# One-core diffusion step with 32 experts: the last expert pair's rows spread over the tokens by a one-hot matmul, the other rows read back during that pair

## The chip, the cores and the metric

The kernel runs on one core of one Trainium2 chip. The metric is device time in microseconds (us), the median of several runs. The core's engines are named as in the profile: PE (TensorE matmul), PEld (its weight loads), DVE (VectorE), ACT (ScalarE), POOL (GpSimd) and SP (SyncE, which here only issues DMAs). Everything is fp32. One fp32 matmul stands in the trace as two MATMUL records, a transpose as one.

## The reference, cut to what matters

384 tokens (128 context, 256 latent) of width 1024 pass two layers. Layer 0 mixes tokens by attention, layer 1 by a Hyena long convolution whose filters are computed from small weights. Each layer ends with a mixture of 32 experts, of which every token uses two. What the change touches is the sum over experts and what follows it:

```
combine = jnp.sum(jax.nn.one_hot(expert_id, N_EXPERTS) * e_w[..., None], axis=1)
a = jnp.einsum('nd,edh->neh', t, w_gate)
b = jnp.einsum('nd,edh->neh', t, w_up)
act = jax.nn.silu(a) * b * combine[:, :, None]
out = jnp.einsum('neh,ehd->nd', act, w_down)
...
x = x + g2 * hierarchical_moe(h, ...)        # then the next layer's RMSNorm, or the final one
```

## The kernel before, in words

**Tokens and experts.** The residual `xT` lies transposed, 8 chunks of 128 features by 384 tokens. The experts are worked in 16 pairs, `q` = 0 to 15; a pair has 128 slots, 64 for each expert, and a slot holds one token of that expert. A table `tab` in SBUF gives each slot its token, its weight and its row of the buffer `yD` in HBM ("expert_rows", 768 rows of 1024: two for each token). A slot with no token has a number out of range. A pair with more than 64 tokens for an expert gets extra windows, run by `extra(q)` under a branch.

**One pair** (`moe` of each engine). PE runs `gate_up` (L849, 16 matmuls of 512 columns), ACT the Silu (L1230), DVE the product `A` (L1655), PE transposes it (L855), DVE copies it (`AT`, L1658), PE runs `down` (L863, 8 matmuls), and ACT and DVE copy the halves of the result to `Y` (L1238, L1667). POOL scatters `Y` to its rows of `yD` by an indirect DMA (`scatter`, L1811) and gathers tokens for later pairs (L1806, L1839). Meanwhile PE turns the next pair's gathered tokens.

**The end of a layer's experts.** After the last pair's scatter SP reads all of `yD` back in eight DMAs of 384 KB (`load_rows`, L429) into `y2`, two rows for each token. Per chunk of features, DVE adds the two rows (L1682, counted by `ysum`), PE transposes the sum (three transposes, L941), DVE adds it, gated, to `xT` (`add_mix`, L1421), ACT squares the new chunk (L1125), and PE adds the square to the norm's sum by a matmul with ones (`norm_sum`, L628). Then ACT takes the root (L1127), DVE the reciprocal (L1389 after layer 0, L1404 at the end of the kernel) and the normalised chunks (L1391, L1406).

**Filters beside the experts, layer 0 only.** The Hyena filters are made in 8 pieces, `f` = 0 to 7, one in every two pairs. SP loads a piece's weights and decays (`load_filter`, L391 to L394); ACT makes the decays (`decay`, L1087, L1094) in even pairs; in odd pairs PE makes the taps in three parts (`taps`, L582), DVE multiplies them by the decay (`tap_decay`, L1357) and forms sums and differences (`tap_sums`, L1363, L1365), ACT takes absolute values (L1100) and POOL adds them (`size_sums`, L1872, L1874); in the next even pair PE makes the spectra in three parts (`spectra`, L599 to L604) and the sizes (`sizes`, L613), and ACT and DVE copy the spectra out. Piece 7 has no next pair: its spectra and sizes stand between the last pair and the residual. The sums and differences lie in `hT`, which the next norm overwrites.

**After layer 0** the Hyena input projection follows: 24 steps of 8 matmuls of 384 columns (L997). Its weights come in six chunks of 2 MB (`load_win`, L434) into the ring where the expert weights were; step `n` uses chunk `n // 4`, and a semaphore stands for one or two chunks (`WIN_GROUP`).

**What sets the order.** Every engine runs its own list in program order, and semaphores join the lists. On SP the end of layer 0 is:

```
sp.wait_ge(sem("gu_mm"), PAIRS - 1)
for n in (0, 1):
    load_win(sp, n)
sp.wait_ge(sem("dn_mm"), 2 * (PAIRS - 1))
load_win(sp, 2)
load_rows(sp, 0)
```

A wait on one list holds all that stands behind it there.

## Time and profile before

| | us |
|---|---|
| three runs, median (lowest to highest) | 1273.88 (1272.04 to 1278.01) |
| the profiled execution, own time | 1280.37 |
| its span, first to last instruction | 1278.5 |
| PE busy in it | 1089.1 (85%) |
| DVE, ACT, POOL busy | 476.8, 257.0, 185.4 |

The profiled execution took 6.5 us longer than the median run, and 1.9 us of it lie around the span. Busy shares average over stages with different limits, so the stages are read one by one: the chain of waits says what ended last in each, the timeline what else ran, and the tables by stage how fast PE's clock and the DMAs were. Times within the trace count from the start of the span.

### The profile page before, as it was taken

Reading aid. Unit: us, or ns where it says so; the run is one execution under the profiler, and the core shown is the slowest. Engines: PE = TensorE matmul, PEld = TensorE weight load, DVE = VectorE, ACT = ScalarE, POOL = GpSimd, SP = SyncE. Lnnn points to the kernel's source line nnn. Section 1 sums busy time; section 2 is a strip of 40 time slices with the busy share of each in tenths; the row PEclk is TensorE's granted clock in tenths of the full one; section 3 lists DMA queues with packets and bytes.
Section 4 is the critical chain, followed back from the end, with each engine's and each line's share of the span. In section 5 each row is a group of like instructions: output and inputs, shape, how many; then the busy total and the mean of one; then the engine's idle time right before and its main releaser. Section 6 shows DMA issues by size and latency. Waiting matters only on the chain.

```text
span 1278.5 us, 14637 instructions
## 1 busy us (share of the span) xinstructions
PE 1089.1 (85%) x5429; PEld 574.4 (45%) x5429; DVE 476.8 (37%) x1014; ACT 257.0 (20%) x498; POOL 185.4 (15%) x209
## 2 busy tenths in 40 slices
PE   5799888987999789999879999989765988878864
PEld 3344555555444234443345565658662422222223
DVE  3355556234233113332263336784540111111116
ACT  2211334022333123223231110000221000000001
POOL 1020000002322023221100002130011222222100
PEclk8899989986999899999889999999967989889997
DMA  9996985532899569999870200505320899999943
GB/s 351 404 322 264 251 294 225 227 132 70 313 395 401 228 238 356 398 406 410 305 286 1 99 1 0 230 1 198 154 94 20 325 413 413 413 412 407 407 161 129
DMA packets 94241, 324.54 MB, mean 254 GB/s; under 512 B 17647, under 2 KB 33423, under 8 KB 77380
## 3 DMA queue, kind: packets, MB, share of 16 engines
q1 hardware_dynamic: 71936, 303.49, 61.3%
q0 software_dynamic: 15504, 13.37, 3.4%
q10 hardware_dynamic: 6708, 6.45, 1.4%
q8 instruction: 58, 0.95, 0.3%
q14 instruction: 35, 0.29, 0.1%
HBM read 333.22 MB, written 30.11 MB: 284 GB/s over the span
## 4 chain that ended last, share of the span: by engine, by line
PE 63%; DMA 19%; DVE 7%; issue 4%; ACT 3%; SPq 3%; POOL 0%; ACTq 0%; another core or an unknown queue 0%; POOLq 0%; DVEq 0%
PE bank L849 15%; DMA ring<-in_moe_w_up 10%; PE bank L997 10%; PE bank L863 6%; PE bank L668 3%; PE bank L1036 3%; PE bank L784 3%; DMA ring<-in_w_ada 3%; DMA hT<-in_hy_log_decay 3%; PE bank L564 3%; PE bank L599 2%; PE bank L1025 2%; PE bank L983 2%; DMA ring<-in_moe_w_down 2%; PE bank L796 2%
## 5 line engine op out<-in xcount | busy, mean ns | idle before, releaser
L849 PE MATMUL bank<-ring,work 128*64 128x512 f32 x1120 | 267.5, 633 | 44.3 <-issue 38.2
L849 PEld LDWEIGHTS bank<-ring,work 128*64 128x64 f32 x1120 | 82.5, 145 | 220.6 <-issue 216.4
L863 PE MATMUL bank<-ring,work 128*64 128x512 f32 x560 | 129.4, 604 | 4.3 <-DVE work L1643 1.5
L997 PE MATMUL bank<-hT,ring 128*128 128x384 f32 x384 | 128.0, 494 | 5.3 <-ACT hT L1134 5.3
L1655 DVE SCALAR_TENSOR_TENSOR work<-bank,work 128x256 f32<-128x256 f32 x32 | 15.5, 484 | 261.3 <-ACT work L1230 248.6
L997 PEld LDWEIGHTS bank<-hT,ring 128*128 128x128 f32 x384 | 74.0, 194 | 58.0 <-issue 9.7
L863 PEld LDWEIGHTS bank<-ring,work 128*64 128x64 f32 x560 | 37.5, 138 | 74.1 <-issue 63.4
L1230 ACT ACTIVATE work<-bank 128x256 f32<-128x256 f32 x32 | 12.3, 383 | 249.8 <-PE bank L849 249.8
L1667 DVE COPY work<-bank 128x512 f32<-128x512 f32 x32 | 22.1, 692 | 106.8 <-PE bank L863 106.8
L1806 POOL DMA_INDIRECT work<-token_vectors,work x28 | 28.7, 1026 | 199.6 <-PE bank L832 185.7
L564 PE MATMUL bank<-ring,condS 128*32 128x256 f32 x768 | 48.6, 408 | 10.0 <-DVE ada L1334 5.5
L1811 POOL DMA_INDIRECT expert_rows<-work x32 | 32.0, 1000 | 114.9 <-DVE work L1667 113.0
L599 PE MATMUL bank<-hT,const 128*128 128x256 f32 x160 | 43.8, 409 | 4.6 <-DVE hT L1365 4.6
L1036 PE MATMUL bank<-work,ring 128*128 128x128 f32 (+1 forms) x256 | 42.2, 327 | 1.7 <-DVE work L1757 1.7
L668 PE MATMUL bank<-hT,ring 128*64 128x384 f32 x256 | 43.0, 489 | 0.0
L784 PE MATMUL bank<-work,ring 128*128 128x384 f32 x128 | 41.5, 487 | 0.7 <-DVE work L1499 0.7
L1270 ACT ACTIVATE work<-bank,pc 128x128 f32<-128x128 f32 (+1 forms) x48 | 17.6, 418 | 119.8 <-PE bank L997 119.8
L1238 ACT ACTIVATE work<-bank 128x512 f32<-128x512 f32 x32 | 19.1, 598 | 111.5 <-PE bank L863 111.5
L1036 PEld LDWEIGHTS bank<-work,ring 128*128 128x128 f32 x256 | 38.4, 190 | 5.5 <-issue 2.1
L1729 DVE TENSOR_SCALAR work<-work,pc 128x385 f32<-128x385 f32 x24 | 11.5, 480 | 76.6 <-ACT work L1270 76.6
L1125 ACT ACTIVATE sq<-xT 128x384 f32<-128x384 f32 x38 | 19.7, 522 | 100.9 <-DVE xT L1421 59.2
L564 PEld LDWEIGHTS bank<-ring,condS 128*32 128x32 f32 x768 | 24.8, 116 | 33.4 <-DVE ada L1334 9.0
(269 smaller groups left out, 1481.5 us busy)
## 6 DMA issues: line engine op xcount, KB each, us to landing
ring<-in_moe_w_gate SPq DMA_DIRECT2D x32, 2048.0 KB
ring<-in_moe_w_up SPq DMA_DIRECT2D x32, 2048.0 KB
ring<-in_moe_w_down SPq DMA_DIRECT2D x32, 2048.0 KB
ring<-in_w_ada SPq DMA_DIRECT2D x24, 2048.0 KB, 12.5
ring<-in_hy_w_in SPq DMA_DIRECT2D x6, 2048.0 KB, 20.4
filter_spectra<-work ACTq DMA_DIRECT2D x8, 768.0 KB
work<-expert_rows SPq DMA_DIRECT2D x16, 384.0 KB, 6.7
ring<-filter_spectra SPq DMA_DIRECT2D x2, 3072.0 KB, 12.1
```

Source lines behind the costliest of these rows:

```text
L564: last = mm(ada_bank(t)[32 * j:32 * j + 32, 0:256], condS[:, 4 * hk + k, :], w[:, k, 256 * j:256 * j + 256], start=(hk == 0 and k == 0), s ...
L599: last = mm(dst, m[:, off:off + P], smdf[:, part if part < 2 else r, c, :], start=(j == 0), stop=(j == len(ops) - 1))
L668: last = mm(bank[m % 2][b * HD:(b + 1) * HD, 0:T], wq[:, k, h * HD:(h + 1) * HD], hT[:, k, :], start=(k == 0), stop=(k == KD - 1))
L784: last = mm(bank[m % 2][:, 0:T], wo[:, k, m * P:(m + 1) * P], oT[:, k, :], start=(k == 0), stop=(k == KD - 1))
L796: last = mm(bank[c][:, 0:NG + NE], hT[:, k, c * P:(c + 1) * P], rout[:, l, k, :], start=(k == 0), stop=(k == KD - 1))
L849: last = mm(bank[2][WIN * j:WIN * (j + 1), :], gt[:, k, WIN * j:WIN * (j + 1)], gu[:, :, j, k, :], start=(k == 0), stop=(k == KD - 1))
L863: last = mm(bank[b + hf][WIN * j:WIN * (j + 1), :], AT[:, k, WIN * j:WIN * (j + 1)], dn[:, j, k, hf * HALF:(hf + 1) * HALF], start=(k == 0 ...
L983: last = mm(b[:, :], m[:, off:off + P], ztok[o][:, c, hf * HALF:(hf + 1) * HALF], start=(j == 0), stop=(j == len(ops) - 1))
L997: last = mm(bank[n % 2][:, 0:T], w[:, k, (n % 4) * P:(n % 4 + 1) * P], hT[:, k, :], start=(k == 0), stop=(k == KD - 1))
L1036: last = mm(bank[4 + m % 2][:, lo:hi], wout[:, k, m * P:(m + 1) * P], st[:, 2, k, a0:a1], start=(k == 0), stop=(k == KD - 1))
L1806: ind(out=G[:, q % 2, :], out_offset=None, in_=hD, in_offset=at_rows(tab[:, 4 * q + 1:4 * q + 2]), bounds_check=T - 1, oob_is_err=False).t ...
L1811: ind(out=yD, out_offset=at_rows(tab[:, 4 * q:4 * q + 1]), in_=Y[:, q % 2, :], in_offset=None, bounds_check=2 * T - 1, oob_is_err=False).t ...
```

## The change

**Rows.** Only 15 pairs scatter. Pair 15's result stays in SBUF, in `Y[:, 1]`. DVE makes a one-hot matrix of 128 slots by 384 tokens from the slots' token numbers (`spread_last`, during pair 13, into `rstd`), and PE spreads the pair's rows over the tokens by one matmul of 384 columns for each chunk of features (`last_rows`). Into the same PSUM bank it adds the other rows by three matmuls with the identity (`other_rows`) in place of three transposes. The chunks take seven banks instead of two. The buffers are moved so that `y2` does not lie over `Y[:, 1]` and `GT`; SP reads the rows back as soon as pair 14's scatter has landed and pair 15's extra windows are done (`rows_done`), and DVE adds the first four chunks of rows before it copies pair 15's result. As pair 15's rows of `yD` are no longer written, POOL first writes zeros over all of it, three DMAs of 1 MB at the start of each layer's experts.

**Filters.** Piece 7's last tap part comes before pair 15's `down`; its sums go to the ring where pair 14's down weights were; `tap_sums` comes after the residual on DVE; spectra parts 0 and 1 after the residual on PE; part 2 and the sizes after step 1 of the input projection. The copies and the store follow in the projection.

**Loads.** SP issues chunk 0, the row read, chunks 1 and 3, waits for the last spectra and sizes, then chunks 2, 4 and 5.

**Root table.** `squares` begins with a Sqrt of one column, which loads ACT's table for it. Some semaphores are merged (`wo_in` and `wout_in` into `proj_in`, `kv_out` into `y_out`).

```
@@ layout
-        Y = ws(5120, 2 * D).rearrange("p (b d) -> p b d", b=2)
-        GT = ws(7168, D).rearrange("p (k s) -> p k s", k=KD)
-        Gx = ws(8192, D)
...
+        Gx = ws(5120, D)
+        GTx = ws(6144, D).rearrange("p (k s) -> p k s", k=KD)
+        Yx = ws(7168, D)
+        Y = ws(8192, 2 * D).rearrange("p (b d) -> p b d", b=2)
+        GT = ws(10240, D).rearrange("p (k s) -> p k s", k=KD)
...
+        smdf_last = ring[:, 8192:9728].rearrange("p (d t c) -> p d t c", d=2, t=3)
+        RES_BANK = [0, 1, 2, 4, 5, 6, 7]
-        WIN_GROUP = [0, 0, 1, 2, 2, 3]
+        WIN_GROUP = [0, 0, 1, 1, 2, 2]
@@ SP
-            for s in range(2):
-                sp.wait_ge(S_(f"scat{s}_"), B_(f"scat{s}_") + 16 * (PAIRS // 2))
+            sp.wait_ge(S_("scat0_"), B_("scat0_") + 16 * (PAIRS // 2))
+            sp.wait_ge(S_("scat1_"), B_("scat1_") + 16 * (PAIRS // 2 - 1))
+            sp.wait_ge(S_("rows_done"), B_("rows_done") + 1)
...
+            load_win(sp, 0)
+            load_rows(sp, 0)
+            load_win(sp, 1)
+            sp.wait_ge(sem("gu_mm"), PAIRS)
+            load_win(sp, 3)
+            sp.wait_ge(sem("cf_mm"), 3 * NF)
+            sp.wait_ge(sem("size_mm"), NF)
             load_win(sp, 2)
+            load_win(sp, 4)
             sp.wait_ge(sem("dn_mm"), 2 * PAIRS)
             load_win(sp, 5)
@@ PE
+                    if l == 0 and q == PAIRS - 1:
+                        taps(q // 2, 2)
...
+                def last_rows(k):
+                    mm(bank[RES_BANK[k % 7]][:, 0:T], Y[:, 1, k * P:(k + 1) * P], rstd[:, :], start=True, stop=True)
+
+                def other_rows(k):
+                    pe.wait_ge(S_("ysum"), B_("ysum") + k + 1)
+                    for c in range(TC):
+                        last = mm(bank[RES_BANK[k % 7]][:, c * P:(c + 1) * P], y2[:, 0, c, k * P:(k + 1) * P], ident,
+                                  start=False, stop=True, skip_group_check=True)
+                    last.then_inc(S_("res_mm"), 1)
+
+                pe.wait_ge(S_("spread"), B_("spread") + 1)
+                pe.wait_ge(S_("y_set"), B_("y_set") + 2 * PAIRS)
...
+                for k in range(KD - 1):
+                    last_rows(k)
                 for k in range(KD):
+                    if k == 3:
+                        pe.wait_ge(S_("moe_add"), B_("moe_add") + 2)
+                        last_rows(KD - 1)
+                    other_rows(k)
                     if k >= 2:
                         norm_sum(n_norm + 1, k - 2)
                 for k in (KD - 2, KD - 1):
                     norm_sum(n_norm + 1, k)
+                if l == 0:
+                    pe.wait_ge(S_("moe_add"), B_("moe_add") + 2 * KD)
+                    for part in range(2):
+                        spectra(NF - 1, part)
...
+                if n == 1:
+                    spectra(NF - 1, 2)
+                    sizes(NF - 1)
@@ ACT
+                fn(idle[:, :], eps_col[:, :], ACT.Sqrt)
                 for k in range(KD):
                     act.wait_ge(sem(x_set), base + step * (k + 1))
@@ DVE
+                def spread_last():
+                    at = 4 * (PAIRS - 1) + 1
+                    link(v.tensor_copy(mx[:, 0, 0:1], tab[:, at:at + 1]))
+                    for c in range(TC):
+                        link(v.tensor_scalar(mx[:, 1, c:c + 1], mx[:, 0, 0:1], float(PAIRS), float(-c * P * PAIRS), ALU.mult, ALU.add))
+                    for c in range(TC):
+                        last = v.tensor_scalar(rstd[:, c * P:(c + 1) * P], C["slotrow"], mx[:, 1, c:c + 1], None, ALU.is_equal)
+                    last.then_inc(S_("spread"), 1)
...
+                    if l == 0 and q == PAIRS - 1:
+                        tap_decay(q // 2, 2)
+                    if q == PAIRS - 1:
+                        for k in range(KD // 2):
+                            row_sum(k)
                     dve.wait_ge(S_("dn_mm"), B_("dn_mm") + 2 * q + 2)
...
+                for k in range(KD):
+                    add_mix(k, bank[RES_BANK[k % 7]], S_("moe_add"), ada[:, l, 5], S_("res_mm"), B_("res_mm"))
+                    if k < KD // 2:
+                        row_sum(KD // 2 + k)
                 if l == 0:
+                    tap_sums(NF - 1)
@@ POOL
+                pool.wait_ge(S_("g_clear"), B_("g_clear") + 2)
+                for i in range(TC):
+                    pool.dma_start(yD.rearrange("(c p) d -> p c d", p=P)[:, 2 * i:2 * i + 2, :], G).then_inc(S_("zero_in"), 16)
...
-                pool.wait_ge(S_("g_clear"), B_("g_clear") + 2)
+                pool.wait_ge(S_("zero_in"), B_("zero_in") + 48)
...
+                    if q == PAIRS - 1:
+                        nc.gpsimd.nop().then_inc(S_("rows_done"), 1)
...
-                scatter(PAIRS - 1)
```

**How it moves instructions.** A row is a line of the kernel, its operation, output, inputs, output shape and count. On PE, pair 15 of layer 0 and what follows it was, before (gate-up L849, taps L582, spectra L599 to L604, sizes L613, row transposes L941, norm sum L628):

```order
L849 MATMUL bank<-ring,work 64x512 x16
L582 MATMUL bank<-sq,hd 128x512 x2
L855 MATMUL bank<-const,work 128x128 x2
L863 MATMUL bank<-ring,work 64x512 x8
L582 MATMUL bank<-sq,hd 128x512
L599 MATMUL bank<-hT,const 128x256 x6
L602 MATMUL bank<-hT,const 1x256
L599 MATMUL bank<-hT,const 128x256 x4
L604 MATMUL bank<-work,const 1x256
L613 MATMUL bank<-const,hT 128x1 x4
L941 MATMUL bank<-const,work 128x128 x9
L628 MATMUL bank<-sq,const 128x384
```

The same place now (taps L595, down L876, `last_rows` L946, `other_rows` L951, norm sum L641):

```order
L862 MATMUL bank<-ring,work 64x512 x16
L595 MATMUL bank<-sq,hd 128x512 x2
L868 MATMUL bank<-const,work 128x128 x2
L595 MATMUL bank<-sq,hd 128x512
L876 MATMUL bank<-ring,work 64x512 x8
L946 MATMUL bank<-rstd,work 128x384 x7
L951 MATMUL bank<-const,work 128x128 x9
L641 MATMUL bank<-sq,const 128x384
L946 MATMUL bank<-rstd,work 128x384
L951 MATMUL bank<-const,work 128x128 x3
```

The third tap part stands before the down product, the spectra and sizes are gone from here, and seven spread products stand between the down product and the first rows. The spectra (L612, L615, L617) and sizes (L626) stand now, on PE, around the first two steps of the input projection (L1025):

```order
L641 MATMUL bank<-sq,const 128x384 x3
L612 MATMUL bank<-ring,const 128x256 x6
L615 MATMUL bank<-ring,const 1x256
L612 MATMUL bank<-ring,const 128x256 x2
L1025 MATMUL bank<-hT,ring 128x384 x16
L612 MATMUL bank<-ring,const 128x256 x2
L617 MATMUL bank<-work,const 1x256
L626 MATMUL bank<-const,ring 128x1 x4
```

Two parts come before step 0 and the third, with the sizes, after step 1. On SP the end of layer 0 was, before (filter loads L391 to L394, projection weights L434, row read L429):

```order
L391 DMA hT<-in_hy_log_decay 128x256
L393 DMA sq<-in_hy_filt_w 64x256
L394 DMA sq<-in_hy_filt_b 1x256
L434 DMA ring<-in_hy_w_in 128x8x512 x3
L429 DMA work<-expert_rows 128x3x256 x8
L434 DMA ring<-in_hy_w_in 128x8x512 x3
L506 DMA ring<-filter_spectra 128x6144
```

And it is now:

```order
L403 DMA hT<-in_hy_log_decay 128x256
L405 DMA sq<-in_hy_filt_w 64x256
L406 DMA sq<-in_hy_filt_b 1x256
L447 DMA ring<-in_hy_w_in 128x8x512
L442 DMA work<-expert_rows 128x3x256 x8
L447 DMA ring<-in_hy_w_in 128x8x512 x5
L520 DMA ring<-filter_spectra 128x6144
```

One weight chunk stands before the row read instead of three, and five behind it.

## Rows read from the trace of the kernel before

**Rows 1.** Chain of waits, end of layer 0: start us, us, engine and line.
```profile
621.34 5.15 PE bank L863 x16
626.48 1.07 PE bank L582 x2
...
628.30 1.83 DVE hT L1363 x2
...
652.96 0.52 ACT sq L1125
...
655.48 2.56 DVE rstd L1389
```

**Rows 2.** Chain of waits, whole run, input projection.
```profile
659.79 90.71 PE bank L997 x272
751.37 5.16 PE bank L997 x16
```

**Rows 3.** Chain of waits, end of layer 1 and of the kernel.
```profile
1239.22 0.70 DVE work L1667
...
1240.69 2.63 DMA expert_rows<-work
...
1244.85 6.64 DMA work<-expert_rows
...
1260.76 1.28 ACT L1127
...
1262.73 2.56 DVE rstd L1404
```

**Rows 4.** Chain of waits: 12 identity-sized fp32 matmuls; gated add of one chunk.
```profile
998.17 2.68 PE bank L825 x24
...
1256.47 0.74 DVE xT L1421 x2
```

**Rows 5.** Timeline, pairs 14 and 15 of layer 0: start us, us, engine, line, form.
```profile
599.17 1.89 PE L599 MATMUL bank<-hT,const 128*128 128x256 f32 x8
...
607.68 1.13 PE L599 MATMUL bank<-hT,const 128*128 128x256 f32 x4
...
609.30 0.99 POOL L1811 DMA_INDIRECT expert_rows<-work  x1 [14.57 <-DVE work L1667]
...
610.25 7.09 PE L849 MATMUL bank<-ring,work 128*64 128x512 f32 x32
```

**Rows 6.** Timeline, norms: one norm sum; one sum of rows on DVE.
```profile
1258.22 0.81 PE L628 MATMUL bank<-sq,const 128*128 128x384 f32 x2
1258.25 0.55 DVE L1682 TENSOR_TENSOR work<-work 128x384 f32<-128x384 f32 x1
```

**Rows 7.** Busy time by stage: window, us, PE, PEld, DVE, ACT, POOL, clock, DMA, GB/s.
```profile
620.00:624.00 4.00, 3.10 (x10) 1.02 (x12) 1.94 (x4) 0.00 (x0) 0.00 (x0) 0.62 1.06 401
...
632.00:636.00 4.00, 3.88 (x9) 3.16 (x10) 0.07 (x1) 0.06 (x1) 0.65 (x1) 0.50 0.24 66
```

**Rows 8.** The instructions of line L1365: durations ns min/median/max.
```profile
L1365 DVE TENSOR_TENSOR hT<-work x8: 418/2035/2043, 351.3 to 630.0; 128x256 f32<-128x256 f32 x8
```

**Rows 9.** Instructions on expert_rows: landing of its scatters and reads.
```profile
DMA to landing us min/median/max: 2.6/6.3/7.9
```

**Rows 10.** Page, DMA issues: projection weights, KB each, median us to landing.
```profile
ring<-in_hy_w_in SPq DMA_DIRECT2D x6, 2048.0 KB, 20.4
```

**Rows 11.** Timeline of POOL, start of the experts, layers 0 and 1.
```profile
272.82 0.95 POOL L1791 MEMSET work<- 128x1024 f32 x1
...
319.56 1.07 POOL L1845 DMA_INDIRECT work<-token_vectors,work  x1 [3.51 <-DMA work<-slot_table]
...
916.90 0.95 POOL L1791 MEMSET work<- 128x1024 f32 x1
...
962.97 1.07 POOL L1806 DMA_INDIRECT work<-token_vectors,work  x1 [3.23 <-DMA work<-slot_table]
```

**Rows 12.** Timeline, first layer's start: PE's wait for adaLN weights.
```profile
60.30 2.83 PE L564 MATMUL bank<-ring,condS 128*32 128x256 f32 x32 [2.06 <-DMA ring<-in_w_ada]
```

More of the change, by code:

```diff
@@ L346, in build, with smd_of, hsum_of, sabs_of @@
         XT_BANK = [0, 1, 2, 6]
+        RES_BANK = [0, 1, 2, 4, 5, 6, 7]
+        def smd_of(f):
+            return smdf_last if f == NF - 1 else smdf
+        def hsum_of(f):
+            return hsum_last if f == NF - 1 else hsum
+        def sabs_of(f):
+            return sabs_last if f == NF - 1 else sabs
         def chunk_dst(m, lo, hi):
@@ L612, in sizes @@
                         col = 480 + 16 * o + 4 * n + 2 * j + L
-                        last = mm(bank[3][:, col:col + 1], sabs[:, L, j * P:(j + 1) * P], ones[:, 0:1], start=True, stop=True)
+                        last = mm(bank[3][:, col:col + 1], sabs_of(f)[:, L, j * P:(j + 1) * P], ones[:, 0:1], start=True, stop=True)
                 last.then_inc(sem("size_mm"), 1)
@@ L923, in moe @@
                     down(s, 4, S_("dn_mm"))
-                    if l == 0 and q % 2 == 1:
+                    if l == 0 and q % 2 == 1 and q < PAIRS - 1:
                         taps(q // 2, 2)
@@ L1242, in moe @@
                             store_spectra(q // 2 - 1)
-                    if l == 0 and q % 2 == 1:
+                    if l == 0 and q % 2 == 1 and q < PAIRS - 1:
                         sizes(q // 2)
-                if l == 0:
-                    spectra(NF - 1)
-                    store_spectra(NF - 1)
             moe(0, 1)
@@ L1252, in _ @@
             modulate(2, 1, 0)
+            spectra(NF - 1)
             def z_copy(o, g):
@@ L1732, in _ @@
                     .then_inc(sem("conv_done"), 1)
+                if n == 1:
+                    spectra(NF - 1)
+                if n == 3:
+                    filter_sizes()
                 for g in Z_TURNS_AFTER.get(n, ()):
```

84 lines of the change are left out of this document (34 added, 50 removed).

## Prediction

> **What bounds the kernel now.** I read the chain of waits first, because the change works at two ends that only the chain shows: the end of layer 0's experts and the end of the kernel. The timeline and the table by stage come second, to see what runs beside the chain there and at which clock.
>
> At the end of the kernel the chain is a plain relay [rows 3]: DVE's copy of the last pair starts at 1239.22, its rows are scattered to HBM (2.63 us), all rows are read back (6.64 us), and only then come the sums. The reciprocal of the last norm starts at 1262.73, so 23.5 us after the copy. PE does no products for the experts in that time.
>
> At the end of layer 0 the chain goes another way [rows 1]. The same scatter and read run, but the chain runs over the filters' last piece: the third tap part (626.48), sums on DVE (1.83 us for two, at 628.30), spectra and sizes on PE, and then the residual, whose last add ends at 652.96. The reciprocal starts at 655.48 and the input projection at 659.79 [rows 2]. From the start of the last down product (621.34) to the projection that is 38.5 us. Part of it is slow clock: in the 4 us from 632 PE has 0.50 of its clock, which is 1.2 GHz of 2.4, after it stood still [rows 7]. The projection starts slow too: its first 17 groups take 90.71 us, where a group at full clock takes 5.16 us, so 87.7 for 17 [rows 2]. 3.0 us are lost there.
>
> **The change part by part.**
>
> *New end of the experts, both layers.* The pieces on PE, at full clock:
> - A 384-column product takes 5.16 / 8 = 0.645 us [rows 2]. Seven come before the first rows: 4.5 us; the eighth 0.65.
> - The other rows of a chunk are three 128-column fp32 products. Twelve such take 2.68 us [rows 4], so 0.67 for a chunk and 5.4 for eight. Three transposes were cheaper, a record each instead of two.
> - Five norm sums stand before the last chunk's rows: 5 x 0.645 = 3.2 us.
>
> That makes 13.75 us on PE. Before it stands the copy (0.70 [rows 3], with a hand-over 0.74), behind it the last gated add (0.74 [rows 4]), its square (0.52 [rows 1]), its norm sum (0.81 [rows 6]) and the root. The root's table load is gone from here: after the load ended at 1260.76 + 1.28 = 1262.04 the root and hand-over took 0.69 to the reciprocal [rows 3]. The sum is 0.74 + 13.75 + 0.74 + 0.52 + 0.81 + 0.69 = 17.25 us from the start of the copy to the reciprocal. DVE's list would take 8 x 0.74 + 4 x 0.55 = 8.1 us [rows 4, 6] against PE's 9.25 after the first seven products, so PE paces it; if the two overlapped better than I lay them out, DVE's pace would give back 1.1 us in each layer.
>
> *Layer 1 alone:* 23.5 - 17.25 = **6.3 us less**. The sums of the first four chunks must not hold the copy: on DVE they stand ahead of it. Pair 14's scatter is issued about when pair 15's gate-up begins (609.30 and 610.25 in layer 0 [rows 5]); that gate-up of 7.09 us, the steps to the down product and that product lie between. Landing of scatters and reads has a median of 6.3 us and a maximum of 7.9 [rows 9], so a scatter and the read of the first columns take some 12 us and end about when the down product does. I put nothing for it.
>
> *Layer 0.* Four terms.
> 1. The third tap part now stands before the down product, and waits for the first tap multiply: about 0.7 on DVE (the size of the copy in [rows 3]) and 1.07 on PE [rows 1], 1.8 us. In return the down product begins later on a clock that is rising (0.62 in the 4 us from 620 [rows 7]), and it took 5.15 us at that clock. I take 1.3, between 0.7 and 1.8. The copy, which follows the down product's end at 626.49, starts at 627.8.
> 2. POOL's adds of absolute values now fall on the row sums that stand before the copy. One DVE sum of 256 columns took 418 ns once and 2035 ns in the median, when POOL's adds ran [rows 8]; so 0 to 1.6 us, and I take 0.8: copy at 628.6. By the Trainium skill, SBUF — State Buffer, section "Practical consequences" of its port rules, a VectorE instruction with two SBUF inputs blocks against a GpSimd one that reads SBUF, and one with a single SBUF input does not; by that the copy from PSUM itself is not held, and the sum stays; without it the copy could be held as well, which would add up to 1.6 us to the sum.
> 3. The residual's last add then ends at 628.6 + 0.74 + 13.75 + 0.74 = 643.8, against 652.96. DVE's sums for the last spectra follow: 1.83 [rows 1] + 0.42 (uncontended, [rows 8]) = 2.25 us. The root is ready after 0.52 + 0.81 + 0.69 = 2.0, so the sums cost the reciprocal 0.25: it starts at 646.1. From reciprocal to projection it is 659.79 - 655.48 = 4.3 us, so 650.4. Beside it PE runs spectra parts 0 and 1: 1.89 for the first [rows 5], as much for the second and 0.6 for its extra product, 4.4 us from 646.1, so 650.5. Both end together; the projection starts at 650.5, **9.3 us** earlier.
> 4. PE has then been busy up to the start, so I expect the full clock and the 3.0 us back. Part 2 and the sizes go into the projection, which PE bounds: 610.25 - 607.68 = 2.6 us [rows 5].
>
> Layer 0: 9.3 + 3.0 - 2.6 = **9.7 us less**.
>
> *Loads.* The row read of layer 0 starts after pair 14's scatter, issued at 609.30 [rows 5]: landed by 612 to 617, the first halves of the read by 615 to 625 [rows 9], while DVE needs them from 624 to 627. I put nothing, with the upper bound in the rivals. Behind it come projection chunks 1 and 3; two chunks at the 401 GB/s of [rows 7] take 10.5 us, well before 650. Chunks 2, 4 and 5 are issued at about 663 and step 8 needs chunk 2 at 650.5 + 2.6 + 8 x 5.16 = 694; landing took 20.4 us [rows 10], so about 10 us are spare.
>
> *Zeros.* POOL's first gather waits for 3 MB of zeros. Between the end of the memsets and that gather lie 45.8 us in layer 0 and 45.1 in layer 1 [rows 11]; 3.1 MB at some 400 GB/s are 8 us, twice that beside weight loads. What is queued behind on POOL, the slot table's scatter and read, needs the router's result, which DVE makes meanwhile. Nothing.
>
> *Root table at the first norm.* There the load (1.28 us, with its one-column Sqrt about 1.4) stands before the squares, so PE's first products start 1.4 later. But PE then waits 2.06 us for adaLN weights at 60.30 [rows 12], which covers PE's own delay. Nothing, and 1.4 at worst, if those weights are late by as much. The Trainium skill, ScalarE: Activation LUTs, "What ACT_TABLE_LOAD costs", gives 2.66 us for a switch, load and drain, which would make that bound 2.8; the trace shows 1.28 and the next instruction 0.7 later, so I keep 1.4. In the other norms the load lies under waits.
>
> Pair 13's one-hot (seven small DVE instructions) lies under the next gate-up of 7.09 us [rows 5].
>
> **The sum.** 6.3 + 9.7 = 16.0 us. The profiled execution's own 1280.37 us would be 1264.4; on the median of the runs shown, 6.5 us lower, it is 1273.88 - 16.0 = **1258 us**.
>
> **The rivals.**
> - *The first norm pays.* The request for the next adaLN weights waits for PE's first products, and if it comes 1.4 us late, so may those weights. Against it speak the 2.06 us only if PE's part alone is late. It gives 1259.4. By the skill's price it would be 1260.7.
> - *The read holds DVE in layer 0.* The row sums stand ahead of the copy on DVE, and everything hangs on the copy. The DMAs are full there (401 GB/s), and a projection chunk takes 20.4 us to land. Were the read as slow, from 617 to 637 or 638, the copy would start some 9 us late: 1267. For it: that load; against: 7.9 us was the longest of its own kind.
> - *The clock stays low.* If PE's waits in the new end are long enough for the clock to fall, the 3.0 us stay lost and the spread takes longer: 1261 to 1264.
> - *Slower: the zeros hold POOL.* A wait of the gathers takes the place of the wait removed. The slowest landing on that buffer, 7.9 us for 0.5 MB [rows 9], is 66 GB/s; at that rate 3.1 MB take 48 us and end 2 or 3 us after the gathers want to start, in each layer. The change turns to a loss where they take over 53 us (8 us late, twice). At 50 GB/s it is 63 us, 17 late in each layer: 1258 + 35 = 1293. Against it: those landings are of single scatters, whose fixed part counts in full, and the zeros go in order.
>
> That the change would not do what it says I can exclude for the order: the one-hot, the read and the spectra stand where the diff puts them.
>
> **How the numbers follow.** Forecast 0.60; first norm 0.14; read holds DVE 0.14 (about half of it less than 0.5% below the time before); clock 0.07; zeros 0.05. A measurement of this kernel can tell about 0.5%, 6.4 us, from no change. Faster by more: 0.60 + 0.14 + 0.07 + 0.07 = 0.88; the same: the other 0.07; slower: 0.05. The low end: the lowest run shown is 1.8 under the median, DVE's pace gives 2.2, the POOL collision 0.8 and the tap part 0.6: 1252. The high end takes in the first two rivals: 1267.
>
> **What would show it.** Right: no scatter and no read between the last copy and the last norm; seven products of 384 columns right after the copy, at full clock; reciprocal 17 us after the copy in layer 1 and the projection about 29 us after the start of pair 15's transposed product in layer 0; no table load there. Wrong: a DVE wait for the row read ahead of the last copy; a POOL wait for the zeros ahead of the first gather; a longer wait at the projection's steps 8 or 16.

## The result, and the profile after

The change makes the kernel faster, by less than forecast: 1264.93 us (median of 13 runs) against 1273.88 for the kernel before (13 runs beside them). The ratio is 0.9924, 95% interval 0.9906 to 0.9942, which is 9.7 us (7.4 to 12.0) where 16 were forecast; the two medians alone differ by 9.0. A second set of timings gave 0.9942 (0.9920 to 0.9963), 7.4 us. One later run of the kernel before took 1783.98 us at a granted clock of 0.59 and enters no comparison. The profiled execution took 1264.05 us, span 1262.2. It lies near its median, while the one of the kernel before lay 6.5 us over its own; so the difference of the two spans, 16.3 us, is not the gain.

**End of layer 0.** The chain of waits of the changed kernel (start us, us, engine and line), to set beside [rows 1, 2]:

```profile
616.87 2.08 PE bank L595 x2
618.94 5.92 PE bank L876 x16
624.86 0.84 issue
625.70 4.75 PE bank L946 x14
...
640.10 0.74 DVE xT L1455 x2
640.84 1.73 DVE ring L1397 x2
...
647.47 11.35 PE bank L1025 x32
...
661.19 77.51 PE bank L1025 x240
```

The scatter, the read, the last tap sums and the first spectra are gone from between the down product and the adds. The seven one-hot products (L946, two records each) follow the copy, the last add ends at 640.84, and the projection starts at 647.47, 28.5 us after the start of the down product (38.5 before; the forecast was about 29). The clock is full there, as the table by stage shows (window, us, PE, PEld, DVE, ACT, POOL, clock, DMA share, GB/s), where [rows 7] had 0.50:

```profile
632.00:636.00 4.00, 3.86 (x24) 2.90 (x23) 3.76 (x10) 1.89 (x4) 0.00 (x0) 1.00 0.92 336
```

**End of layer 1.** The same view, to set beside [rows 3]:

```profile
1215.04 3.63 DMA expert_rows<-work
...
1220.15 6.29 DMA work<-expert_rows
...
1226.94 0.55 DVE work L1697
1227.49 0.67 DVE work L1723
...
1228.29 4.75 PE bank L946 x14
1233.04 0.68 PE bank L951 x6
...
1235.19 0.88 PE bank L641 x2
...
1245.67 2.56 DVE rstd L1438
```

The chain still runs through a scatter and a read, but they are pair 14's, and they lie beside pair 15. The last sum ahead of the copy (L1697) ends 0.05 to 0.1 us after the down product does. So the copy was held by almost nothing here, though the view names the read; in the second profile of the changed kernel it starts 0.3 us after the down product's end, held by the read (run 7 has the other profiles). From the copy (1227.45) to the reciprocal (1245.67) it is 18.2 us, against 23.5 before and 17.25 forecast.

**The front.** The chain of the first norm:

```profile
18.05 0.10 ACT condS L1107
...
18.17 1.28 ACT L1147
...
29.67 1.91 PE bank L577 x32
...
31.59 0.37 SPq L394
...
46.50 16.62 DMA ring<-in_w_ada
...
63.16 3.05 PE bank L577 x32
```

The root's table load stands on the chain, as the first rival had it: behind it come the squares, PE's first adaLN products, SP's requests that wait for those, and the weights, which PE gets at 63.16 instead of 60.30 [rows 12].

**The zeros.** POOL's timeline (start us, us, engine, line, form, idle time before and its releaser) in layer 0:

```profile
274.95 2.16 POOL L1851 DMA_DIRECT2D expert_rows<-work  x3 [0.30 <-POOL work L1848]
305.05 1.06 POOL L1855 DMA_INDIRECT slot_table<-pay,idx  x1 [27.94 <-DVE pay L1625]
...
319.96 1.08 POOL L1905 DMA_INDIRECT work<-token_vectors,work  x1 [3.24 <-DMA work<-slot_table]
```

The page's DMA issues give the zeros 15.8 us to land:

```profile
expert_rows<-work POOLq DMA_DIRECT2D x6, 1024.0 KB, 15.8
```

In layer 0 the last of them lands at 293.1, 11.9 us before the first request for the slot table; in layer 1 it is 8.5 us before. The first gather waits for the slot table, and starts 0.4 us later than in [rows 11].

### The profile page after: what moved, and what is told of

Same layout as the page of the kernel before. It is cut to its first block, busy times and chain, and to the rows that moved or that the text cites. A ratio compares the mean times of both kernels' runs of the same rounds, so it can differ in the third digit from the quotient of the medians.

```text
span 1262.2 us, 14809 instructions
## 1 busy us (share of the span) xinstructions
PE 1096.0 (87%) x5509; PEld 580.6 (46%) x5509; DVE 478.0 (38%) x1028; ACT 257.5 (20%) x503; POOL 187.4 (15%) x213
## 4 chain that ended last, share of the span: by engine, by line
PE 67%; DMA 19%; DVE 5%; issue 4%; ACT 3%; SPq 2%; POOL 0%; ACTq 0%; POOLq 0%; DVEq 0%
PE bank L862 15%; DMA ring<-in_moe_w_up 12%; PE bank L1025 10%; PE bank L876 6%; PE bank L681 3%; PE bank L1067 3%; PE bank L797 3%; DMA ring<-in_w_ada 3%; PE bank L577 3%; PE bank L612 2%; PE bank L1056 2%; PE bank L1011 2%; DMA ring<-in_moe_w_down 2%; PE bank L809 2%; PE bank L838 2%
## 5 line engine op out<-in xcount | busy, mean ns | idle before, releaser
L862 PE MATMUL bank<-ring,work 128*64 128x512 f32 x1120 | 268.1, 634 | 42.2 <-issue 36.1
L876 PE MATMUL bank<-ring,work 128*64 128x512 f32 x560 | 130.2, 608 | 3.7 <-DVE work L1677 1.5
L1025 PE MATMUL bank<-hT,ring 128*128 128x384 f32 x384 | 126.3, 488 | 0.0
L1025 PEld LDWEIGHTS bank<-hT,ring 128*128 128x128 f32 x384 | 72.2, 190 | 51.9 <-ACT hT L1166 2.3
L876 PEld LDWEIGHTS bank<-ring,work 128*64 128x64 f32 x560 | 37.7, 139 | 75.5 <-issue 65.6
L1067 PE MATMUL bank<-work,ring 128*128 128x128 f32 (+1 forms) x256 | 42.2, 327 | 1.7 <-DVE work L1814 1.7
L1847 POOL MEMSET work<- 128x2048 f32 x2 | 3.6, 1806 | 240.2 <-DVE xT L1455 183.8
## 6 DMA issues: line engine op xcount, KB each, us to landing
expert_rows<-work POOLq DMA_DIRECT2D x6, 1024.0 KB, 15.8
```

What stands on the lines that cost most here:

```text
L862: last = mm(bank[2][WIN * j:WIN * (j + 1), :], gt[:, k, WIN * j:WIN * (j + 1)], gu[:, :, j, k, :], start=(k == 0), stop=(k == KD - 1))
L876: last = mm(bank[b + hf][WIN * j:WIN * (j + 1), :], AT[:, k, WIN * j:WIN * (j + 1)], dn[:, j, k, hf * HALF:(hf + 1) * HALF], start=(k == 0 ...
L1025: last = mm(bank[n % 2][:, 0:T], w[:, k, (n % 4) * P:(n % 4 + 1) * P], hT[:, k, :], start=(k == 0), stop=(k == KD - 1))
L1067: last = mm(bank[4 + m % 2][:, lo:hi], wout[:, k, m * P:(m + 1) * P], st[:, 2, k, a0:a1], start=(k == 0), stop=(k == KD - 1))
```

## The experiments

For all runs I compare stretches of the program, since two profiles of the kernel before alone differ by 7.4 us in their spans. Each number is the difference of two start times in the trace of that run, or runs from the start or to the end of its span.

| stretch, us | before | before again | changed | changed again | turned, added |
|---|---|---|---|---|---|
| second Silu to first square | 0.10 | 0.10 | 1.62 | 1.62 | 0.10 |
| start to attention's out-projection | 228.72 | 224.83 | 229.60 | 228.83 | 228.37 |
| attention's out-projection to pair 15's gate-up, layer 0 | 381.53 | 378.43 | 376.93 | 379.49 | 378.44 |
| pair 15's gate-up to projection | 49.54 | 48.97 | 40.86 | 40.92 | 35.94 |
| of it, copy to reciprocal | 28.95 | 29.11 | 18.17 | 18.18 | 14.00 |
| projection to hyena's out-projection | 211.44 | 211.46 | 212.02 | 212.05 | 212.05 |
| pair 15's gate-up to the end, layer 1 | 52.02 | 52.28 | 47.49 | 47.06 | 42.96 |
| of it, copy to reciprocal | 23.51 | 23.74 | 18.22 | 18.21 | 14.07 |

**1. The kernel before, profiled again.** No edit.

> The kernel before, profiled a second time, unchanged. My theory: its first profiled execution (1280.37 us, 6.5 over the median of its timed runs) was slow by chance in stretches that the change doesn't touch, above all the start of layer 0's experts (3.7 us, with a 1.9 us wait of DVE at 311.94 that PE's end doesn't explain). Then a second profile lies within 2 us of 1273.9, the time from the start of the out-projection of attention to the first gate-up of layer 0 is 3 to 4 us shorter (82.5 instead of 86.2), and the two tails that the change touches stay as they were: from pair 15's gate-up to the projection 49.5 us in layer 0, from pair 15's gate-up to the end 52.0 us in layer 1, both within 1 us. Rival: the stretches outside the tails are the same in every execution of the kernel before (within 0.5 us), the change itself shortens them, and 16 us was the right size for this execution: then the second profile shows 86 us again there.

The median is 1271.2 us, the profiled execution took 1272.97, span 1271.1. With no change made, the stretch from attention's out-projection to pair 15 is 3.1 us shorter and the front ahead of it 3.9 us, while both tails agree within 0.6 us with the first profile. From the out-projection to the first gate-up it is 84.2 us, 2.0 less than in the first profile, where I expected 3 to 4. One wait shows where 1.9 us of the 3.1 lay. This is DVE's copy for the first pair, in the timeline of the first profile of the kernel before:

```profile
311.94 0.69 DVE L1627 COPY work<-bank 128x512 f32<-128x512 f32 x1 [3.42 <-remote]
```

and in its second profile:

```profile
306.13 0.69 DVE L1627 COPY work<-bank 128x512 f32<-128x512 f32 x1 [1.49 <-PE bank L825]
```

The theory holds in kind: the surplus of the first profile was chance, and lies outside the tails. More than half of the 7.4 us lies in the front, where the change adds the table load, so gains and costs there can't be read from one profile of each kernel.

**2. The changed kernel again.** No edit.

> The changed kernel once more, unchanged, with a second profile. My theory, from the segments of the eight profiles so far: against the kernel before, from pair 15's gate-up to the projection 8 to 10 us less in layer 0 (39.4 to 41.0 us against 49.0 to 49.5), from pair 15's gate-up to the end 3.4 to 5.3 us less in layer 1 (47.0 to 49.1 against 52.0 to 52.3), 0.55 us more in the projection, up to 2 us more at the front; 10 to 12 us in all, ratio 0.990 to 0.9925. Rival, the sum of the prediction: 16 us, ratio 0.9875.

1265.07 us, ratio 0.9942 (0.9920 to 0.9963). The stretches come out as expected: 8.0 to 8.7 us less in layer 0, 0.6 more in the projection, 4.5 to 5.2 less in layer 1. The timed gain, 7.4 us (4.7 to 10.2), is under the 10 to 12 expected. The sum of 16 us lies outside both intervals.

**3. No early table load at the first norm.**

```
+                if n > 0:
-                fn(idle[:, :], eps_col[:, :], ACT.Sqrt)
+                    fn(idle[:, :], eps_col[:, :], ACT.Sqrt)
```

> The changed kernel, with the root's table loaded ahead at the four later norms only. My theory: at the first norm the load is 1.28 us on the chain, because ACT goes from the second Silu straight to the first square; without it the first square follows the second Silu within 0.1 us, and the root's load (1.28 us) begins at the last square's end and stands out behind PE's last product by 0.3 to 0.4 us, as in the kernel before. The first product of the ada weights then starts 0.9 us nearer to the first Silu, and so do the arrival of the last w_ada transfer that is asked for in the first 35 us (63.1 in the changed kernel) and the first q/k projection: 0.9 us less in all, ratio to the kernel before 0.9917 against the 0.9924 of the changed one. Rival, that of the prediction: PE's idle time of 2.06 us ahead of the ada products hides the load, and all of the 2.9 us shift at the front was chance: then the arrival of w_ada does not move against the first Silu, and the time is that of the changed kernel.

1260.54 us, ratio 0.9905 (0.9879 to 0.9930). The first square follows the Silu at once, and the load stands between last square and root (timeline of ACT):

```profile
16.93 0.20 ACT L1107 ACTIVATE condS<-pc 128x8 f32<-128x8 f32 x1
17.03 0.92 ACT L1158 ACTIVATE sq<-xT 128x384 f32<-128x384 f32 x2
...
24.33 1.28 ACT L1160 ACT_TABLE_LOAD   x1
```

The weights arrive at 59.1 instead of 63.2, and against the second Silu 42.2 us after it instead of 45.2. The direction is the theory's; the size, 3 us, is more than the 0.9 expected, and the clock has a share in it (the squares' products took 7.7 us here and 8.8 in the changed kernel, where PE had stood idle for 3.72 us ahead of them instead of 2.44, and the granted clock was 0.50 from 20 to 26 us; here it was back at 1.00 from 21). Run 5 bears on the rest. The two intervals of the ratio overlap; the trace decides here, not the time.

**4. No early load at all.**

```
-                fn(idle[:, :], eps_col[:, :], ACT.Sqrt)
```

> The changed kernel without any of the five early loads of the root's table. My theory: the load comes back between last square and root at the two layer ends and at the end of the kernel; there the last square and PE's last product end about 0.8 to 1.0 us apart (1243.98 and 1244.9 in the changed kernel), so that 0.3 to 0.5 us of the 1.28 stands out at each of the norms 2 and 4, and up to 0.5 at the norms 1 and 3, against 0.9 us gained at the first norm: between -0.9 and +0.9 us against the changed kernel, +0.1 as one number; copy of pair 15 to reciprocal in layer 1: 18.6 instead of 18.2. Rival: the whole load of 1.28 us stands out at each layer end, as the prediction's sum had it in its steps: 19.5 there, and +1.6 to +4 us in all.

1260.62 us, ratio 0.9913 (0.9886 to 0.9939). Copy to reciprocal is 18.5 us in both layers instead of 18.2, so an early load at a layer's end is worth 0.3 us and not 1.28 (18.6 were expected). The timeline of the end shows why:

```profile
1237.47 2.46 PE L641 MATMUL bank<-sq,const 128*128 128x384 f32 x6
...
1238.45 0.52 ACT L1156 ACTIVATE sq<-xT 128x384 f32<-128x384 f32 x1 [0.79 <-DVE xT L1454]
1238.99 1.28 ACT L1158 ACT_TABLE_LOAD   x1
1240.29 0.58 ACT L1158 ACTIVATE rstd<-bank,eps_col 128x384 f32<-128x384 f32 x1
```

The load starts as soon as the last square is done, beside the product that the root waits for. It sticks out by 0.3 us.

**5. The Silu table loaded ahead instead.** As run 3, and:

```
             act.wait_ge(sem("preset"), 3)
+            fn(idle[:, :], eps_col[:, :], ACT.Silu)
             act.wait_ge(sem("pc_done"), 1)
```

> The changed kernel without the root's early load at the first norm, and with one Silu on a spare element before ACT waits for the parameters, so that the table that it needs is loaded while ACT is idle. My theory: the first Silu then starts with DVE's copy of the parameters instead of 1.28 us behind it, and the first square 0.3 us behind that copy instead of 1.5 (0.1 and 1.28 in the kernel before, 1.6 and 1.28 in the changed one); the first ada products come 1.3 us earlier against that copy than in the run without the first early load, and 2.2 us earlier than in the changed kernel. In all 1.3 us less than without the first early load, 2 to 3 us less than the changed kernel: ratio to the kernel before about 0.990 (0.9865 to 0.992). Rival: the last w_ada transfer is bound by the queue of loads and not by the products that free its place; then its arrival does not move and the gain ends in TensorE's idle time ahead of it: 0 us.

1262.98 us, ratio 0.9902 (0.9879 to 0.9925), against 0.9905 in run 3: no gain over it. The ratio lies in the range that the theory gave, but no timing here can tell 1.3 us; by the trace the theory falls and its rival holds. The chain of waits:

```profile
25.11 0.37 SPq L394
...
26.07 7.95 SPq L469
...
44.63 15.17 DMA ring<-in_w_ada
...
59.84 1.93 PE bank L577 x32
```

PE's first products are over at 25.1 instead of 28.0 (run 3), but one of SP's requests (L469) takes 7.95 us to issue instead of 4.41, and the request for the adaLN weights that PE waits for next goes out at 44.15 instead of 43.48. In all twelve profiles it goes out between 43.5 and 44.2 where the first products end before 29.3, eight times; and 14.4 to 15.3 us after them where they end at 30.6 to 31.6, four times (45.5 to 46.1). Those four all have the early load. So the front has a floor that the queue sets, the kernel before stood on it, and the early load lifts it off in four of six runs: 1.3 us in the mean (45.1 for the six profiles with the load, 43.8 for the six without). Attention's out-projection starts 1.4 us later in the mean of the same six (227.6 against 226.2), but each six spread over 3 to 5 us there.

**6. The zeros written twice.** A second pass behind the first:

```
+                pool.wait_ge(S_("zero_in"), l * 96 + 48)
+                for i in range(TC):
+                    pool.dma_start(yD.rearrange("(c p) d -> p c d", p=P)[:, 2 * i:2 * i + 2, :], G).then_inc(S_("zero_in"), 16)
...
-                pool.wait_ge(S_("zero_in"), B_("zero_in") + 48)
+                pool.wait_ge(S_("zero_in"), B_("zero_in") + 96)
```

> The changed kernel, with the row buffer zeroed twice in each layer, one pass after the other (3.1 MB more for each layer, and POOL waits for the first pass before it issues the second). My theory: zeros cost nothing: POOL issues them at 274.95 and has no other work until 305.05, one pass lands in 15.8 us, and so two are over by about 307; the weights of the first pairs are asked for early enough. Expected: 0 to +1.5 us against the changed kernel (part of it POOL's wait at 305), and the first gate-up of layer 0 unmoved within 0.5 us. Rival: they share the transfer rate of about 415 GB/s with the weights that the first pairs wait for, and 3.1 MB at that rate are 7.6 us: then each layer's first gate-up comes up to 7 us later and the kernel takes up to 15 us more, and the one pass in the changed kernel would have eaten as much of its gain.

1262.80 us, ratio 0.9927 (0.9902 to 0.9953), the same as the changed kernel. POOL's timeline, layer 0:

```profile
271.87 2.16 POOL L1851 DMA_DIRECT2D expert_rows<-work  x3 [0.30 <-POOL work L1848]
290.10 2.10 POOL L1854 DMA_DIRECT2D expert_rows<-work  x3 [16.08 <-DMA expert_rows<-work]
301.97 1.07 POOL L1858 DMA_INDIRECT slot_table<-pay,idx  x1 [9.77 <-DVE pay L1625]
```

POOL waits for the first pass and is still 9.8 us early. From the out-projections to the first gate-up it is 82.1 and 100.1 us (82.5 and 100.0 in the changed kernel). The zeros cost nothing, and the rival that had them hold POOL is out.

**7. Row sums behind the copy.**

```
-                    if q == PAIRS - 1:
-                        for k in range(KD // 2):
-                            row_sum(k)
...
                     v.tensor_copy(Y[:, s, HALF:D], bank[5][:, :]).then_inc(S_("y_set"), 1)
+                    if q == PAIRS - 1:
+                        for k in range(KD // 2):
+                            row_sum(k)
```

> The changed kernel, with the row sums of the first half of D moved behind DVE's copy of pair 15's output in both layers (ahead of it in the changed kernel). My theory: their place costs and gives nothing. Four sums are 4 x 0.52 = 2.1 us, and TensorE has 4.75 us of products with the one-hot tile after the copy before it asks for the first sum; so copy to reciprocal stays at 18.2 us in both layers (within 0.3), and the copy starts at most 0.1 us earlier after the down product's end, since the sums held it 0.05 us in the changed kernel. In layer 0 the sums then no longer run beside POOL's adds, where two of them took 1.89 us instead of 1.03. Total: that of the changed kernel within what can be measured. Rival: sums ahead of the copy are 2.1 us of DVE time that each tail saves: copy to reciprocal 20.3 and 4 us more in all. Second rival: the read holds the copy, and moving the sums gives up to 1 us at each end.

1262.77 us, ratio 0.9910 (0.9889 to 0.9931). Copy to reciprocal is 18.18 and 18.22 us, within 0.01 of the changed kernel. The timeline of layer 1 shows the room:

```profile
1225.81 1.96 DVE L1697 TENSOR_TENSOR work<-work 128x384 f32<-128x384 f32 x4
1226.04 4.75 PE L946 MATMUL bank<-rstd,work 128*128 128x384 f32 x14 [0.89 <-DVE work L1720]
```

All four sums are done before PE is halfway through the one-hot products. So the hoisted sums are neither a gain nor a cost in these profiles. In others they do hold the copy. Of the sixteen layer ends in the eight profiles that have the sums ahead of it, the copy starts 0.05 us after the down product's end in eleven, and 0.2 to 0.9 us after it in five; the longest is layer 0 of run 10, where the down product ends at 623.50 and the copy starts at 624.44, behind sums that ran beside POOL's adds.

**8. The read of layer 1 held back.** As run 7, and in the row loads:

```
             sp.wait_ge(S_("rows_done"), B_("rows_done") + 1)
+            if l == 1:
+                sp.wait_ge(S_("y_set"), B_("y_set") + 2 * PAIRS)
```

> As the run with the sums behind the copy, and in layer 1 SP waits for the copy of pair 15's output before it reads the other rows back (in the changed kernel it reads them during pair 15). Nothing else of the old tail returns: there is no store of pair 15's rows to wait for. My theory: in the kernel before, the stretch from copy to reciprocal was the store (about 1.5 us to its issue, 3.6 us to land), the read and then 24 transposes with their sums; of what the change removed, most of the read's time is hidden in this tail too, beside the 4.75 us of products with the one-hot tile. The first quarter lands some 6 us after its issue, so the first sum is there about 7 us after the copy starts, against 5.4 us where TensorE asks for it: copy to reciprocal in layer 1 grows from 18.2 to about 20.2 us (19 to 21.5). Layer 0 as in the other run. Rival: the read during the pair is the whole of the gain, and the product only pays for itself: then copy to reciprocal goes back to 23.5 us or more.

One execution, 1266.86 us. Copy to reciprocal in layer 1 is 23.1 us; I expected 20.2, and the rival 23.5. The timeline of DVE:

```profile
1230.78 1.03 DVE L1699 TENSOR_TENSOR work<-work 128x384 f32<-128x384 f32 x2 [4.53 <-DMA work<-expert_rows]
...
1234.13 1.03 DVE L1699 TENSOR_TENSOR work<-work 128x384 f32<-128x384 f32 x2 [2.32 <-DMA work<-expert_rows]
...
1236.41 0.56 DVE L1699 TENSOR_TENSOR work<-work 128x384 f32<-128x384 f32 x1 [0.59 <-DMA work<-expert_rows]
```

The first quarter lands 4.4 us after the request (1226.35), which the one-hot products do cover; the second and third come 3.3 and 2.3 us behind, and the rest of the tail goes at their pace. Some 1.5 us of the delay are slow clock, behind PE's waits for the rows: on the chain of waits a norm sum, the eighth one-hot product and a chunk's products with the identity took 1.13, 1.28 and 1.28 us instead of 0.88, 0.65 and 0.67, and the granted clock beside them was 0.50 (columns as in [rows 7]):

```profile
1238.00:1240.00 2.00, 2.00 (x9) 1.62 (x7) 1.20 (x4) 0.70 (x2) 0.00 (x0) 0.50 0.00 0
```

By this one execution the gain of the change in this tail is the read's time, and the clock that is low behind it (0.50 from 1244 to 1248 in the kernel before, too), taken out from behind the copy. With the store dropped and the read left behind the copy, 0.4 to 0.6 us remain (23.1 against 23.5 and 23.7): the product and the dearer sums take about what the store did.

**9. The two parts turned round.** The other rows are transposed into the banks first, three of eight chunks before the copy, and the one-hot product is added:

```
+                def other_rows(k):
+                    pe.wait_ge(S_("ysum"), B_("ysum") + k + 1)
+                    for c in range(TC):
+                        tr(bank[RES_BANK[k % 7]][:, c * P:(c + 1) * P], y2[:, 0, c, k * P:(k + 1) * P], ident)
...
+                    mm(bank[RES_BANK[k % 7]][:, 0:T], Y[:, 1, k * P:(k + 1) * P], rstd[:, :], start=False, stop=True,
+                       skip_group_check=True).then_inc(S_("res_mm"), 1)
```

> The changed kernel, with the order of the two parts of the last sum turned round: the other rows are transposed into the banks first (as the kernel before did: 3 instructions, 0.49 us for each k), three of the eight while TensorE waits for the copy of pair 15's output, and the products with the one-hot tile are added to them; in the changed kernel the products come first and the other rows are added by products with the identity, 6 instructions and 0.83 us for each k. My theory: TensorE bounds this tail. After the copy it has 3 x 0.65 + 5 x (0.47 + 0.65 + 0.65) = 10.8 us up to the last sum's square instead of 14.4: copy to reciprocal 14 to 15 us instead of 18.2 in both layers, 6.5 to 8.5 us less in all; ratio to the kernel before 0.986 to 0.988. Rival: DVE bounds it (8 adds of 0.74, 4 sums of 0.55 between them, and ACT's squares behind each add): then TensorE only waits in other places, and copy to reciprocal falls to 16.5 to 17.5, 1.5 to 3.5 us less in all.

1254.41 us, ratio 0.9859 (0.9834 to 0.9884); copy to reciprocal 14.00 and 14.07 us. PE paces this tail, as the theory has it. The kernel leaves part of the sum out. The Trainium skill, PSUM — Partial Sum Buffer, "The four PSUM rules", has it that what starts a bank anew clears the marks of the whole bank, and a later product without start overwrites where the mark is clear. By that rule the product replaces two of the three transposed pieces of each bank. Run 10 agrees: with only the first piece starting the bank, the sum is whole.

**10. Turned, and added.** As run 9 and run 3, with the transposes as

```
+                        mm(bank[RES_BANK[k % 7]][:, c * P:(c + 1) * P], y2[:, 0, c, k * P:(k + 1) * P], ident,
+                           start=(c == 0), stop=True, is_transpose=True, skip_group_check=True)
```

> As the run with the turned order, without the early load at the first norm, and with one difference in the eight sums: of the three transposes into a bank only the first one starts the bank anew, so that the product with the one-hot tile is added to all three (in the earlier run each of the three started it anew, and the product replaced what the first two had left). My theory: the time of the tail doesn't change by that: copy to reciprocal 14.0 to 14.1 us in both layers, as in that run, and the front as in the run without the first early load: 1253 to 1256 us, ratio to the kernel before 0.984 to 0.987, some 7 to 9 us less than the changed kernel. Rival: transposes that leave the bank open have to follow the product in order and can't run ahead as before: 0.3 us more for each k, copy to reciprocal 16 us or more.

1254.84 us, ratio 0.9859 (0.9838 to 0.9880): 17 to 18 us less than the kernel before, and 10 less than the changed one beside it, where 7 to 9 were expected. Here the sum is whole, and this is the version that beats both. The timeline of PE in layer 1:

```profile
1223.77 1.20 PE L948 MATMUL bank<-const,work 128*128 128x128 f32 x9
...
1224.81 2.10 PE L952 MATMUL bank<-rstd,work 128*128 128x384 f32 x6
...
1231.61 0.49 PE L948 MATMUL bank<-const,work 128*128 128x128 f32 x3
```

Nine transposes run while PE waits for the copy, and each later chunk needs three records (0.49 us) where the product with the identity needed six (0.83).

## Why the prediction was right, and where it was not

The direction and the mechanism were right, and the time fell into the range. The size was too large: 16.0 us against 9.7 timed. The stretches give 8.4 - 0.6 + 4.9 - 1.3 = 11.4 us (means of two profiles each, the front from twelve). Nearly the same tails are 39.4 to 41.1 us in layer 0 and 47.0 to 49.1 in layer 1 over these two profiles and those of runs 3 to 7, and with all seven the sum is 11.0. What lies between that and the timed 9.7 and 7.4 stays open. So does how layer 0's gain divides between the rows and the filters: no run moves the one without the other.

- *Layer 0, terms 1 to 3: 9.3 us forecast, 8.0 to 8.7 measured.* From pair 15's gate-up to the copy the forecast had 18.35 us (610.25 to 628.6), and it is 18.4, which is luck: two errors of 0.8 us cancel. The down product was to begin "on a clock that is rising"; from 618 to 622 the granted clock was 0.50, and it took 5.92 us instead of 5.15 (the tap part ahead of it, 2.08 us for its two records, is slow too). And the 0.8 us put for POOL was not paid. POOL's adds did fall on the row sums, as these rows of DVE and POOL show:

```profile
620.33 1.03 DVE L1697 TENSOR_TENSOR work<-work 128x384 f32<-128x384 f32 x2 [0.66 <-DMA work<-expert_rows]
...
621.27 1.80 POOL L1933 TENSOR_TENSOR ring<-work 128x768 f32<-128x768 f32 x1 [14.53 <-ACT work L1131]
622.60 1.89 DVE L1697 TENSOR_TENSOR work<-work 128x384 f32<-128x384 f32 x2 [1.24 <-DMA work<-expert_rows]
```

  Two sums took 1.89 us beside POOL's add and 1.03 alone, 0.9 us more; the forecast put 0.8. But the down product ended at 624.86 and the copy began at 624.91, so nothing of it was paid here (in run 10 it was: see run 7). The Trainium skill, SBUF — State Buffer, "Practical consequences", has a DVE instruction with two SBUF inputs contend with a GpSimd one that reads SBUF, and the sums agree. That a copy from PSUM is not held, as the prediction took from there, these rows of the same trace show: wholly beside POOL's add it took the 0.69 us that it takes elsewhere.

```profile
354.21 1.84 POOL L1933 TENSOR_TENSOR hT<-work 128x768 f32<-128x768 f32 x1
354.91 0.69 DVE L1661 COPY work<-bank 128x512 f32<-128x512 f32 x1
```

  A DVE wait for the row read ahead of the copy, which the prediction named as a sign of its being wrong, did come (0.66 and 1.24 us), and cost nothing in this profile for the same reason.
- *Layer 0, term 4: a gain of 0.4 us forecast, a loss of 0.6 measured.* The step that failed is "I expect the full clock and the 3.0 us back". The clock was full, but the first two steps (32 records) took 11.35 us where 10.32 were laid out, so 1.0 of the 3.0 stayed lost at the full clock. The trace shows where. The first step's products begin at 647.40, 648.18, 649.06, 649.94 and 650.81, up to 0.88 us apart instead of 0.645. Each after the first begins 0.05 us after ACT has made its input, with two activations for a chunk and five chunks in 4.50 us:

```profile
646.26 4.50 ACT L1166 ACTIVATE hT<-hT,ada,amul 128x128 f32<-128x128 f32 x10 [3.28 <-DVE hT L1425]
```

  So at the full clock ACT, not PE, paces these products, and the prediction's 3.0 us took PE's pace from the first one on. The inserted spectra and sizes took 2.4 us (2.6 forecast).
- *Layer 1: 6.3 us forecast, 4.5 to 5.2 measured.* The working is right in kind, and its 17.25 us are short by 1.0, mostly in hand-overs. The seven products took 4.75 us and not 4.5, the first norm sum 0.88, and PE waited 0.14 for it: 14.4 us on PE instead of 13.75. The wait ahead was 0.84 (0.74 forecast), and add, square, sum and root took 3.0 (2.76). That makes 18.2 instead of 17.25. Behind the reciprocal another 0.1 to 0.8 us went.
- *Table load at a layer's end.* "The root's table load is gone from here" was right, but run 4 shows it worth 0.3 us.
- *The first norm.* "PE then waits 2.06 us for adaLN weights" [...] "which covers PE's own delay", with nothing put for it, failed. PE's wait was no cover, because the request for those weights itself hangs on PE's first products. That was the first rival, at 0.14; it cost 1.3 us in the mean (its price was 1.4). The load and its one-column Sqrt moved the first square by 1.52 us, near the bound of 1.4 that the prediction took from the trace. By the Trainium skill, ScalarE: Activation LUTs, "What ACT_TABLE_LOAD costs", it had set 2.8 beside it; the measurement decides for the smaller one.
- *Loads, zeros.* Right at nothing: run 6 for the zeros, and 240 records of the projection in 77.51 us, 5.17 a group of 16, without a wait for weights.
- *The base.* The sum was made against a profiled execution 6.5 us over the median. Its span was 7.4 us longer than that of the second profile, 3.1 of it in a stretch that the change leaves alone and 3.9 in the front (run 1). The prediction subtracted from the median, which was the right way; taken from the spans, 16 would have looked exact.

## What to carry to other kernels

An idle engine covers a delay only if what it waits for was asked for by someone else: follow the request back, and if it hangs on the engine that you delay, the delay comes through. When a store and read are replaced by a product, price what is left by its records (an fp32 product is two, a transpose one), and put the part that doesn't need the late operand first. Profile the kernel before twice before a sum of several small terms is compared with a difference of spans.

## What the runs showed of the hardware

- ACT's table load does not wait for what its activation waits for: in run 4 it starts at 1238.99, right behind the last square, and runs 1.28 us beside the product that the root needs. A load placed ahead by hand at a layer's end gained 0.3 us (copy to reciprocal 18.2 us instead of 18.5), and at the first norm, where ACT had nothing to wait for, it moved the first square by 1.52 us.
- A transpose into one bank, written as a matmul that starts the bank only with the first of three pieces, can be followed by an fp32 product that adds to all three, at 0.65 us for 384 columns on the chain of waits of run 10, as in the changed kernel.
- SP's requests can themselves be the bound: the one for the key cache (L469) took 7.95 us to issue when asked for at 26.07 (run 5), 4.41 at 28.95 (run 3) and 2.98 at 33.04 (the changed kernel). In the eight profiles where it was asked for between 26.1 and 30.9 it ended at 33.4 to 34.0; in the other four, from 32.3 to 33.0 on, at 35.5 to 36.1.
- DVE's sum of two SBUF rows is slower beside POOL's add (two took 1.89 us instead of 1.03 in the changed kernel, layer 0), and DVE's copy from PSUM is not (0.69 us beside it and elsewhere).
